# Alternating two attentions of one layer in one pipeline, stick-breaking by sigmoids and running products in the softmax pipeline, and head norm inside the output projection

## The chip, the cores and the metric

The kernel runs on one core of a Trainium2 chip. The time is the device time of one execution in microseconds (us). Before the change three executions gave 2448.42, 2451.39 and 2452.55, so the median is 2451.39. The core has five engines that run their own instruction lists in order and meet only at semaphores: TensorE (PE) for matmuls and transposes, VectorE (DVE), ScalarE (ACT), GpSimd (POOL), and SyncE (SP), which issues the transfers.

## The reference

A sequence of 512 tokens with 1024 features passes a first block (window attention with RWKV, then a gated feed-forward part) and two more layers. Each of these has a mixer, an output projection with a residual, and a feed-forward part. Layer 0 has the even mixer, layer 1 the odd mixer. Only the mixers and the projections behind them matter here.

```python
# even mixer: 8 forgetting heads (64 wide), 4 differential heads (values 128 wide)
s = q @ k.T * scale + (c[q] - c[k]);  p = softmax(causal(s));  o_a = p @ v
p = softmax(causal(q1 @ k1.T * scale)) - lam * softmax(causal(q2 @ k2.T * scale))
o_b = rms_norm_2(p @ v, subln) * (1.0 - lam_init)      # per head: x*rsqrt(mean(x*x)+EPS)*g
out = concatenate([o_a, o_b]) @ w_out

# odd mixer: 8 heads over keys picked by an indexer (softmax), 8 stick-breaking heads
z = q @ k.T * scale;  mask = key < query
log1m = where(mask, log_sigmoid(-z), 0)
after = reverse_cumsum(log1m) - log1m
a = where(mask, exp(log_sigmoid(z) + after), 0);  o_d = a @ v
out = concatenate([o_c, o_d]) @ w_out
```

## The kernel before

Everything lies in SBUF with features on the 128 partitions and tokens along the free axis (S = 512, P = 128, HD = 64). Weights stream in as fp32 tiles (`raw`), which ACT copies to a rounded part (`whi`, L309) and POOL subtracts to a rest (`wlo`, L313). Each product with weights is then three matmuls (L326 to L328). The program is a row of stages. In a stage each engine has a list written out by hand, and a stage ends with a handover by the engines' sequencers.

`attend` (L1020) runs attention over units. A unit is one pair of maps (two heads, or the two maps of one differential head) and one block of 128 queries; its keys are the blocks up to its own, so the width w goes 128, 256, 384, 512 and starts again. There are 16 units for 8 heads in pairs, or for 4 differential heads. In iteration i the engines do this, in this order:

- PE: scores of unit i (L1066), once the fused step of i-2 has left that pair of banks. Then it multiplies the weights of unit i-4 by the values (L1078), once ACT has copied them. Then it transposes the weights of unit i-3 (L1089), once they are normalised and the same copy is made.
- DVE: for forgetting units a masking add on the last block (L1102), then for each map a fused step that adds the bias, scales and takes the row maximum (L1106). Then the reciprocal of unit i-1's row sums (L1112), for differential units the merge of the two maps of i-2 (L1118), and the copy of a finished output (L1123).
- ACT: two exponentials of unit i (L1134), then the copy of unit i-3's transposed weights out of PSUM (L1143).
- POOL: normalises both maps of a unit (L1043), or, for a differential unit, scales the second map (L1048).

Even mixer (`even_mixer`, L2017): first 16 forgetting units, then as another stage 16 differential units, whose outputs go to `ob`. Then `norm` (L420) as a stage of its own: squares on ACT (L432), means by matmuls with a column of ones (L393), square root and reciprocal, spreading by matmuls (L402), and two DVE steps per head (L2054, L2055) into `oT`. Then `project_out` (L717), whose `Cut` (L546) splits the eight slices of `oT` (L554 on ACT, L559 on DVE) before eight output tiles follow, each of 24 matmuls and a residual add (L772). The feed-forward part follows.

Odd mixer (`odd_mixer`, L2196): PE makes keys and values from the latent (L2227, L2230), ACT and DVE copy them out (L2246). One `attend` of 16 units follows. `turn` (L1145) transposes the values of the stick-breaking heads. `stick_breaking` (L2257) then works head by head on blocks of keys by queries, 1280 columns in all: scores (L2282) copied out by ACT (L2319), softplus from three passes on ACT over 1280 columns (L2322 to L2324) and one on DVE (L2354), the running sum over keys by matmuls with a triangle and with ones (L2292, L2294), subtraction and clamp (L2347, L2349), exponential (L2328), masking (L2356, L2361), values (L2303) and copy (L2333). `project_out` then begins again with the split.

## Time and profile before

The profiled execution took 2450.87 us; its span in the profile is 2449.0 us. All times of the trace count from the start of that span. The mean granted clock of PE was 0.953.

| stretch | from | to | us |
|---|---|---|---|
| forgetting units | 1164.55 | 1222.56 | 58.0 |
| differential units | 1222.56 | 1270.06 | 47.5 |
| head norm, up to the first split of `project_out` | 1270.06 | 1287.40 | 17.3 |
| `project_out` of the even layer up to its last residual add's start | 1287.40 | 1335.52 | 48.1 |
| picked-key softmax units | 1871.1 | 1922.0 | 50.9 |
| transposes of the stick-breaking values | 1922.0 | 1927.0 | 5.0 |
| stick-breaking | 1927.0 | 2013.2 | 86.2 |

Over the whole span PE is busy 92% of the time, DVE 50%, POOL 40% and ACT 35%. The rows further down are of four kinds. A timeline row has a start, a duration (both us), the engine, the line, what is written and read, and a count; in brackets stands how long the engine was idle before and what released it. A row of the view by windows has a stretch, its length, busy time and count for PE, PEld (weight load), DVE, ACT and POOL, then the granted clock (1 is full), the share of the DMA engines and GB/s. A row of the groups by line has the count, busy time and mean duration, and the idle time before. A row of the view of one line has shortest, median and longest duration in ns, and first and last start.

### The profile page before, as it was taken

What the parts mean: (1) busy time and instruction counts of PE and PEld (TensorE: products, weight loads), DVE (VectorE), ACT (ScalarE), POOL (GpSimd) and SP (SyncE); (2) the same over time, 40 slices, a digit from 0 to 9 for tenths busy, and PEclk for the clock granted to TensorE, in tenths of its full rate; (3) what the DMA queues carried; (4) which work ended last, traced back from release to release, by engine and by line L of the source; (5) the groups of instructions that cost most, each with busy time, mean ns of one, the idle gap of its engine ahead of it and who ended that gap; (6) DMA issues with size and microseconds to landing.
All of it is one profiled execution on the core that took longest, in us unless ns stands there. A gap on an engine that the chain in (4) does not pass through costs nothing. (4 is left out here: it accounts for less than half of the span.)

```text
span 2449.0 us, 35685 instructions
## 1 busy us (share of the span) xinstructions
PE 2250.8 (92%) x13345; PEld 1805.7 (74%) x13345; DVE 1230.1 (50%) x2004; ACT 869.4 (35%) x1337; POOL 973.3 (40%) x507
## 2 busy tenths in 40 slices
PE   6995997799999999899778999999998799999998
PEld 4674986588788888777567888877786557888876
DVE  3337425777406761515453677711695362677601
ACT  3443223433213332432543333322324563333322
POOL 4322111344444444466523344444466204344442
PEclk8996998899999999999778999999999899999999
DMA  4220011233323333233002233233231003233332
GB/s 127 61 61 15 4 33 47 60 102 95 102 82 96 90 102 103 66 86 86 1 1 80 76 102 94 84 95 105 73 87 44 1 1 95 78 103 94 90 94 82
DMA packets 347229, 177.16 MB, mean 72 GB/s; under 512 B 20851, under 2 KB 344302, under 8 KB 347118
## 3 DMA queue, kind: packets, MB, share of 16 engines
q1 hardware_dynamic: 346620, 175.53, 25.1%
q8 instruction: 74, 1.21, 0.2%
q14 instruction: 37, 0.30, 0.0%
q10 hardware_dynamic: 210, 0.08, 0.0%
q0 software_dynamic: 288, 0.03, 0.0%
HBM read 173.51 MB, written 2.11 MB: 72 GB/s over the span
## 5 line engine op out<-in xcount | busy, mean ns | idle before, releaser
L313 POOL TENSOR_TENSOR wlo<-raw,whi 128x1024 fp32r<-128x1024 f32 (+3 forms) x347 | 793.9, 2292 | 1226.3 <-ACT whi L818 645.2
L326 PE MATMUL banks<-xhi,whi 128*128 128x512 f32 x1688 | 670.7, 397 | 5.9 <-DVE cb L977 3.9
L328 PE MATMUL banks<-xhi,wlo 128*128 128x512 f32 x1688 | 660.4, 391 | 0.0
L327 PE MATMUL banks<-xlo,whi 128*128 128x512 f32 x1688 | 660.3, 391 | 0.0
L326 PEld LDWEIGHTS banks<-xhi,whi 128*128 128x128 f32 x1688 | 319.2, 189 | 81.9 <-issue 12.7
L327 PEld LDWEIGHTS banks<-xlo,whi 128*128 128x128 f32 x1688 | 319.3, 189 | 69.0 <-issue 3.6
L328 PEld LDWEIGHTS banks<-xhi,wlo 128*128 128x128 f32 x1688 | 318.8, 189 | 67.1
L818 ACT ACTIVATE whi<-raw 128x1024 fp32r<-128x1024 f32 (+1 forms) x216 | 209.7, 981 | 191.6 <-DMA raw<-in_ffn_w_out_dram 84.5
L906 ACT ACTIVATE cb<-banks,conv 128x512 f32<-128x512 f32 x152 | 118.1, 779 | 446.0 <-DVE banks L966 446.0
L326 PE MATMUL banks<-ghi,whi 128*128 128x512 f32 x608 | 238.7, 393 | 19.7 <-DVE xT L1008 13.8
L327 PE MATMUL banks<-glo,whi 128*128 128x512 f32 x608 | 237.2, 390 | 0.0
L328 PE MATMUL banks<-ghi,wlo 128*128 128x512 f32 x608 | 237.1, 390 | 0.0
L966 DVE TENSOR_TENSOR banks<-banks,rs 128x512 f32<-128x512 f32 x152 | 106.3, 700 | 184.9 <-PE banks L328 168.5
L985 DVE CAST ghi<-gv 128x512 f32 (+1 forms) x76 | 168.4, 2216 | 9.0
L326 PEld LDWEIGHTS banks<-ghi,whi 128*128 128x128 f32 x608 | 114.5, 188 | 49.3 <-issue 17.9
L309 ACT ACTIVATE whi<-raw 128x1024 fp32r<-128x1024 f32 (+3 forms) x131 | 128.0, 981 | 34.1 <-PE banks L328 17.6
L328 PEld LDWEIGHTS banks<-ghi,wlo 128*128 128x128 f32 x608 | 114.5, 188 | 24.1
L327 PEld LDWEIGHTS banks<-glo,whi 128*128 128x128 f32 x608 | 114.6, 188 | 23.4
L977 DVE SCALAR_TENSOR_TENSOR cb<-banks,conv,cb 128x510 f32<-128x510 f32 x152 | 113.8, 749 | 18.3 <-DVE cb L975 0.3
L1008 DVE TENSOR_TENSOR xT<-banks,xT 128x512 f32 x16 | 11.1, 692 | 209.1 <-PE banks L328 209.1
L975 DVE SCALAR_TENSOR_TENSOR cb<-banks,conv,cb 128x511 f32<-128x511 f32 x152 | 112.7, 741 | 4.2 <-ACT cb L906 4.2
L1043 POOL TENSOR_SCALAR ex<-ex,mx 128x128 f32<-128x128 f32 (+3 forms) x64 | 68.3, 1085 | 37.6 <-DVE mx L1112 37.6
(446 smaller groups left out, 2730.5 us busy)
## 6 DMA issues: line engine op xcount, KB each, us to landing
raw<-in_ffn_w_in_dram SPq DMA_DIRECT2D x88, 512.0 KB, 3.9
raw<-in_w_ffn_up_dram SPq DMA_DIRECT2D x64, 512.0 KB, 4.1
raw<-in_w_ffn_down_dram SPq DMA_DIRECT2D x32, 512.0 KB, 4.2
raw<-in_ev_w_in_dram SPq DMA_DIRECT2D x25, 512.0 KB, 4.0
raw<-in_ffn_w_out_dram SPq DMA_DIRECT2D x32, 384.0 KB, 3.6
raw<-in_ffn_w_out_dram SPq DMA_DIRECT2D x32, 320.0 KB, 3.2
raw<-in_od_w_in_dram SPq DMA_DIRECT2D x20, 512.0 KB, 3.8
raw<-in_w_in_dram SPq DMA_DIRECT2D x16, 512.0 KB, 3.8
```

The costliest lines, as they stand in the source:

```text
L309: w_hi.by(act.activation(whi[s % CUT][:, 0:n, :], raw[s % RAW][:, 0:n, :], ACT.Copy))
L313: return pool.tensor_tensor(wlo[c][:, 0:n, :], raw[b][:, 0:n, :], whi[c][:, 0:n, :].bitcast(F32), ALU.subtract)
L326: pe.matmul(acc, whi[b][:, k, :], hi(k), start=first and k == 0, stop=False)
L327: pe.matmul(acc, whi[b][:, k, :], lo(k), start=False, stop=False)
L328: mm = pe.matmul(acc, wlo[b][:, k, :], hi(k), start=False, stop=last and k == n - 1)
L818: act.activation(whi[s % CUT][:, 0:n, :], raw[s % RAW][:, 0:n, :], ACT.Copy).then_inc(w_hi.h, 1)
L906: act.activation(cb[j][:, :], bank[j][:, :], ACT.Identity, scale=conv[:, 2, bass.ds(c, 1)], bias=conv[:, 3, bass.ds(c, 1)])\
L966: dve.tensor_tensor(bank[j % 4][:, :], bank[j % 4][:, :], rs, ALU.mult).then_inc(scaled.h, 1)
L975: chain(dve.scalar_tensor_tensor(cb[j][:, 1:S], bank[j][:, 0:S - 1], conv[:, 1, bass.ds(c, 1)], cb[j][:, 1:S], ALU.mult, ALU.add))
L977: dve.scalar_tensor_tensor(cb[j][:, 2:S], bank[j][:, 0:S - 2], conv[:, 0, bass.ds(c, 1)], cb[j][:, 2:S], ALU.mult, ALU.add).then_inc(conve ...
L985: dve.tensor_copy(ghi[:, i * 2 + q, :], gv[q][:, :]).then_inc(upper.h, 1)
L1043: ins = pool.tensor_scalar(e[:, g, 0:w], e[:, g, 0:w], mx[u % 4][:, 2, g:g + 1], None, ALU.mult)
```

## The change

1. Even mixer: one `attend` of 32 units, in which forgetting unit (j, n) and differential unit (j, n) alternate. Values are now multiplied five iterations behind the scores, not four (SUM). A unit's transposed weights always lie in banks 4 and 5. ACT's copy stands at the head of the next iteration (COPY = 4). Differential outputs go straight to `oT`.
2. Head norm: the stage is gone. Inside `project_out` the first two output tiles go slice by slice over `oT`, while the last four slices are squared (DVE), averaged over the partitions by a matmul with a square of ones, put through a logarithm and an exponential (ACT, this gives gain * rsqrt), multiplied (DVE) and split.
3. Odd mixer: the values of the stick-breaking heads are transposed in the stage that makes keys and values. Then one `attend` has the 16 softmax units and 16 stick-breaking units behind them. A stick-breaking unit has queries on the partitions, as the softmax ones do. DVE adds the mask in PSUM, ACT takes sigmoid(-z) and sigmoid(z) straight from PSUM, DVE makes the running product of sigmoid(-z) from the last key to the first (one scan for each head, reading and writing backwards), and POOL multiplies sigmoid(z) by the product of one key further. From there it is transposed, copied and multiplied by the values like the others.

```diff
+    class HeadNorm:
+        TILES = 2
...
+        def mean(self, pe, h):
+            pe.wait_ge(self.squared.h, h + 1)
+            pe.matmul(bank[4 + h][:, :], ones, self.sq[:, h, :], start=True, stop=True).then_inc(self.summed.h, 1)
...
+            for k in range(KD):
+                pe.wait_ge(self.ready.h, k + 1)
+                for m in range(self.TILES):
...
+                for h in {1: [0], 2: [1], 3: [2, 3]}.get(k, []):
+                    self.mean(pe, h)
...
+            for k in range(4):
+                self.upper(act, k)
+            split_hi(act, s0 + AHEAD)
+            act.wait_ge(self.set.h, 2)
+            for h in range(5):
+                if h < 4:
+                    x = self.sq[:, h, :]
+                    act.wait_ge(self.summed.h, h + 1)
+                    chain(act.activation(x, bank[4 + h][:, :], ACT.Ln, scale=1.0 / P, bias=self.const[:, 0:1]))
+                    act.activation(x, x, ACT.Exp, scale=-0.5, bias=self.const[:, 1:2]).then_inc(self.rooted.h, 1)
+                if h >= 1:
+                    act.wait_ge(self.normed.h, h)
+                    self.upper(act, 3 + h)
...
-        SETS, TURN, SUM = 2, 3, 4
+        SETS, TURN, COPY, SUM = 2, 3, 4, 5
...
+                    if x.sticking:
+                        pool.wait_ge(scanned.h, sticks.index(u) + 1)
+                        normed.by(pool.tensor_tensor(e[:, :, 0:w - 1], e[:, :, 0:w - 1], rest[u % 2][:, :, 1:w], ALU.mult))
...
-                        pe.wait_ge(normed.h, u + 1)
-                        free = u if heads == 2 else u - 1
-                        if free >= 1:
-                            pe.wait_ge(ptaken.h, free)
+                        wait_weights(pe, u)
+                        if u >= 1:
+                            pe.wait_ge(ptaken.h, u)
...
+                            for g in range(2):
+                                back = sm[u % 2][:, g, 0:w][:, ::-1]
+                                ins = dve.tensor_tensor_scan(rest[u % 2][:, g, 0:w][:, ::-1], back, back, 1.0, ALU.mult, ALU.min)
+                            scanned.by(ins)
...
+                            z = banks[:, b0:b0 + 2, 0:w]
+                            act.activation(sm[i % 2][:, :, 0:w], z, ACT.Sigmoid, scale=-HD ** -0.5)
+                            ins = act.activation(ex[i % 4][:, :, 0:w], z, ACT.Sigmoid, scale=HD ** -0.5)
...
-            norm(lambda k: ob[:, k, :], 4, 2 * HD, EPS, finish, groups=4)
...
-            stick_breaking(sq_, sk_, sv_, past, after, oT)
```

PE in the even attention. `ak`, `aq`, `vta` belong to forgetting units, `bk`, `bq`, `vtb` to differential ones; `ex` to transpose, `pt` to multiply by values. Before:

```order
L1089 MATMUL banks<-cst,ex_305 128x128 x6
L1066 MATMUL banks<-ak,aq 128x256 x2
L1066 MATMUL banks<-ak,aq 128x128 x2
L1078 MATMUL banks<-pt_307,vta 64x128 x6
L1089 MATMUL banks<-cst,ex_306 128x128 x8
L1066 MATMUL banks<-ak,aq 128x256 x4
L1078 MATMUL banks<-pt_308,vta 64x128 x8
```

and in the changed program:

```order
L1146 MATMUL banks<-cst,ex_307 128x128 x6
L1123 MATMUL banks<-ak,aq 128x128 x2
L1135 MATMUL banks<-pt_312,vtb 128x128 x2
L1146 MATMUL banks<-cst,ex_308 128x128 x3
L1123 MATMUL banks<-bk,bq 128x128 x2
L1135 MATMUL banks<-pt_311,vta 64x128 x6
```

The kinds alternate, and each product with values (now L1135) belongs to a unit that was copied one iteration earlier than before.

ACT from the end of the even attention on. `sq<-ob` are the squares of the norm stage, `hi<-oT` the split, `whi` a weight tile. Before:

```order
L432 ACTIVATE sq<-ob 128x512 x4
L408 ACT_TABLE_LOAD
L408 ACTIVATE st<-st 128x16
L151 UNCONDITIONAL_BRANCH
L751 UNCONDITIONAL_BRANCH
L554 ACTIVATE hi<-oT 128x512 x8
L309 ACTIVATE whi_14<-raw_10 128x1024
```

and in the changed program:

```order
L708 ACTIVATE hi<-oT 128x512 x4
L308 ACTIVATE whi_14<-raw_10 128x1024
L720 ACT_TABLE_LOAD
L720 ACTIVATE headsq<-banks,headconst 128x512
L721 ACT_TABLE_LOAD
L721 ACTIVATE headsq<-headsq,headconst 128x512
L720 ACT_TABLE_LOAD
L720 ACTIVATE headsq<-banks,headconst 128x512
L721 ACT_TABLE_LOAD
L721 ACTIVATE headsq<-headsq,headconst 128x512
L708 ACTIVATE hi<-oT 128x512
```

The logarithm (L720) and the exponential (L721) each have a table load in front, for each of the four heads, and the fifth split stands behind two heads' worth of them.

DVE in stick-breaking. Before, one head in its steady state:

```order
L2347 TENSOR_TENSOR aw_479<-zs_474,banks 128x512
L2349 TENSOR_SCALAR aw_479<-aw_479 128x512
L2347 TENSOR_TENSOR aw_479<-zs_474,banks 128x384
L2349 TENSOR_SCALAR aw_479<-aw_479 128x384
L2347 TENSOR_TENSOR aw_479<-zs_474,banks 128x256
L2349 TENSOR_SCALAR aw_479<-aw_479 128x256
L2347 TENSOR_TENSOR aw_479<-zs_474,banks 128x128
L2349 TENSOR_SCALAR aw_479<-aw_479 128x128
L2354 SCALAR_TENSOR_TENSOR sp_478<-zs_475,sp_478 128x1280
L2356 TENSOR_TENSOR sp_478<-sp_478,past 128x128 x4
```

and in the changed program two units:

```order
L1158 TENSOR_TENSOR banks<-banks,own 128x2x128
L1179 SCALAR_TENSOR_TENSOR rest_455<-sm_443 128x384 x2
L1194 COPY oT<-banks 128x128
L1158 TENSOR_TENSOR banks<-banks,own 128x2x128
L1179 SCALAR_TENSOR_TENSOR rest_456<-sm_444 128x512 x2
L1194 COPY oT<-banks 128x128
```

The listing names the scans of L1179 by their operand form. A unit's mask comes one iteration ahead of the scans of the unit before it.

## Rows read from the trace of the kernel before

**Rows 1.** View by windows: forgetting units, differential units, stick-breaking.

```profile
1161.90:1222.60 60.70, 44.85 (x337) 31.49 (x336) 28.94 (x116) 30.55 (x81) 34.19 (x32) 0.78 0.00 1
1222.60:1270.10 47.50, 36.85 (x216) 27.59 (x216) 27.20 (x112) 24.70 (x80) 13.04 (x16) 0.79 0.00 1
...
1926.90:2010.50 83.60, 74.80 (x281) 46.15 (x282) 49.67 (x136) 57.57 (x72) 0.00 (x0) 0.94 0.00 1
```

**Rows 2.** Timeline, forgetting units: two period marks, and one link of the chain.

```profile
1184.38 0.44 PE L1089 MATMUL banks<-cst,ex 128*128 128x128 f32 x2
...
1189.19 0.92 PE L1066 MATMUL banks<-ak,aq 64*128 64x256 f32 x8
...
1190.16 0.43 DVE L1102 TENSOR_TENSOR banks<-banks,mask 128x256 f32<-128x256 f32 x1 [0.86 <-PE banks L1066]
1190.63 0.56 DVE L1106 CUSTOM_DVE_ANT_0 sm<-banks,f 128x384 f32<-128x384 f32 x1
...
1191.71 0.61 ACT L1134 ACTIVATE ex<-sm,mx 128x384 f32<-128x384 f32 x1 [0.85 <-DVE mx L1106]
...
1192.92 1.00 ACT L1143 ACTIVATE pt<-banks 128x1024 f32<-128x1024 f32 x1
...
1193.97 1.09 PE L1078 MATMUL banks<-pt,vta 128*64 128x128 f32 x16
...
1195.00 0.44 PE L1089 MATMUL banks<-cst,ex 128*128 128x128 f32 x2
```

**Rows 3.** Timeline, transposes of differential units: two period marks.

```profile
1240.05 0.27 PE L1089 MATMUL banks<-cst,ex 128*128 128x128 f32 x1
...
1249.10 0.27 PE L1089 MATMUL banks<-cst,ex 128*128 128x128 f32 x1
```

**Rows 4.** Groups by line: the copies of the forgetting, then the differential stage.

```profile
L1143 ACT ACTIVATE pt<-banks 128x256 f32<-128x256 f32 (+3 forms) x16 | 11.1, 692 | 9.8 <-PE banks L1089 9.7
...
L1143 ACT ACTIVATE pt<-banks 128x128 f32<-128x128 f32 (+3 forms) x16 | 6.8, 423 | 6.2 <-PE banks L1089 6.2
```

**Rows 5.** Timeline: first and last period mark of the forgetting units, and last copy.

```profile
1169.06 0.33 PE L1089 MATMUL banks<-cst,ex 128*128 128x128 f32 x1
...
1208.06 0.44 PE L1089 MATMUL banks<-cst,ex 128*128 128x128 f32 x2
...
1269.77 0.29 DVE L1123 COPY ob<-banks 128x128 f32<-128x128 f32 x1 [3.32 <-PE banks L1078]
```

**Rows 6.** Timeline: head norm and the start of the even layer's output projection.

```profile
1272.57 1.28 ACT L408 ACT_TABLE_LOAD   x1
...
1287.40 3.23 ACT L554 ACTIVATE hi<-oT 128x512 fp32r<-128x512 f32 x6 [8.91 <-PEq L151]
...
1290.32 0.63 PE L326 MATMUL banks<-hi,whi 128*128 128x512 f32 x1
```

**Rows 7.** Timeline, odd layer: last period mark, value transposes, start of the output projection.

```profile
1908.32 0.44 PE L1089 MATMUL banks<-cst,ex 128*128 128x128 f32 x2
...
1922.37 3.65 PE L1157 MATMUL banks<-cst,sv 128*128 128x128 f32 x16 [0.66 <-PEq L151]
...
2013.51 3.23 ACT L554 ACTIVATE hi<-oT 128x512 fp32r<-128x512 f32 x6 [0.28 <-PEq L151]
```

**Rows 8.** View of one line each: scan, residual add, addition of two SBUF tiles, POOL product.

```profile
L1246 DVE TENSOR_TENSOR_SCAN tmp<-inside,cs x4: 1224/1224/1226, 192.1 to 197.0; 128x512 f32<-128x512 f32 x4
...
L772 DVE TENSOR_TENSOR xT<-banks,xT x8: 691/692/692, 1297.4 to 1335.5; 128x512 f32<-128x512 f32 x8
...
L614 DVE TENSOR_TENSOR bk<-bk,rotated x3: 692/2696/2698, 1149.0 to 1161.6; 128x512 f32<-128x512 f32 x3
...
L650 POOL TENSOR_TENSOR bk<-bk,rs x4: 1265/1298/1307, 1140.2 to 1159.7; 128x512 f32<-128x512 f32 x4
```

**Rows 9.** Timeline of POOL and DVE at the same moment, two inputs in SBUF each.

```profile
1148.27 2.85 POOL L313 TENSOR_TENSOR wlo<-raw,whi 128x1024 fp32r<-128x1024 f32 x1
...
1148.97 2.70 DVE L614 TENSOR_TENSOR bk<-bk,rotated 128x512 f32<-128x512 f32 x1
```

More of the change, by code:

```diff
@@ L719, in project_out @@
+    def project_out(oT, scale, mixed=None, make_side=None, gain=None):
         s0, n = state["s"], KD
@@ L741, in _ @@
             def _(pe):
-                for m in range(n):
+                if gain:
+                    lead.pe(pe, s0)
+                for m in range(lead.TILES if gain else 0, n):
                     s = s0 + m
@@ L752, in _ @@
             def _(act):
-                lead.act(act)
+                if gain:
+                    lead.act(act, s0)
+                else:
+                    lead.act(act)
                 for m in range(n):
-                    split_hi(act, s0 + m + AHEAD)
+                    if not gain or m >= AHEAD:
+                        split_hi(act, s0 + m + AHEAD)
                     if m >= 3:
@@ L766, in _ @@
                 chain = Chain(dve, dve_chain)
-                lead.dve(dve, None)
+                if gain:
+                    lead.dve(dve)
+                else:
+                    lead.dve(dve, None)
                 for m in range(n + 1):
@@ L1069, in _ @@
                     if 0 <= u < U:
-                        values = units[u][3]
+                        x = units[u]
                         pe.wait_ge(ptaken.h, u + 1)
@@ L1073, in _ @@
                             pe.wait_ge(otaken.h, u - 1)
-                        last = len(values) - 1
-                        for b, v in enumerate(values):
-                            for g in range(heads):
-                                r0, r1 = (g * HD, (g + 1) * HD) if heads == 2 else (0, P)
+                        last = len(x.values) - 1
+                        for b, v in enumerate(x.values):
+                            for g in range(x.heads):
+                                r0, r1 = (0, P) if x.paired else (g * HD, (g + 1) * HD)
                                 mm = pe.matmul(bank[6 + u % 2][r0:r1, 0:P], v[:, r0:r1], pt[u % 2][:, g, b * P:(b + 1) * P],
@@ L1103, in _ @@
-                        if i >= 2:
-                            dve.wait_ge(exped.h, i - 1)
-                        for g in range(2):
-                            ins = dve.tensor_tensor_reduce(sm[i % 2][:, g, 0:w], bank[b0 + g][:, 0:w], bias[g], -HD ** -0.5,
-                                                           3e38, ALU.add, ALU.min, mx[i % 4][:, 0, g:g + 1])
-                        ready.by(ins)
+                        if x.bar is not None:
+                            z = banks[:, b0:b0 + 2, w - P:w]
+                            ins = dve.tensor_tensor(z, z, x.bar.rearrange("p (o n) -> p o n", o=1).broadcast_to([P, 2, P]), ALU.add)
+                            if x.sticking:
+                                barred.by(ins)
+                            else:
+                                chain(ins)
@@ L1110, in _ @@
                     if 0 <= u < U:
[L1111 to L1118 removed]
+                        x, w = units[u], units[u].w
@@ L2246, in _ @@
                             act.activation(dv[:, t, :, :].rearrange("p m n -> p (m n)"), bank[4 + t][:, :], ACT.Copy)
+                        for t in range(NT):
+                            act.wait_ge(flipped.h, t + 1)
+                            act.activation(vt[:, t, :, :].rearrange("p m n -> p (m n)"), bank[t][:, :], ACT.Copy)
                 units = []
@@ new lines, in odd_mixer @@
+                        units.append(Unit([(cq[p0:p0 + HD, j, n * P:w], dk[p0:p0 + HD, j, 0:w]) for p0 in (0, HD)], w,
+                                          [dv[:, b, j, :] for b in range(n + 1)], oT[:, j, n * P:w],
+                                          bias=[future[:, :] if n == 0 else keep[:, n - 1, 0:w]] * 2))
+                for j in range(4):
+                    for n in range(NT):
+                        w = (n + 1) * P
+                        units.append(Unit([(sq_[p0:p0 + HD, j, n * P:w], sk_[p0:p0 + HD, j, 0:w]) for p0 in (0, HD)], w,
+                                          [vt[:, b, j, :] for b in range(n + 1)], oT[:, 4 + j, n * P:w],
+                                          bar=own[:, :], sticking=True))
```

371 lines of the change are left out of this document (136 added, 235 removed).

## The prediction

> **What bounds the kernel now.** I looked first at the busy shares: PE works 92% of the span, so whatever does not touch the stages where PE waits can be worth little. The view by windows then shows where it waits: PE is busy for 44.85 of 60.7 us in the forgetting units, at a mean clock of 0.78, and for 36.85 of 47.5 us in the differential ones. In stick-breaking it is busy for 74.80 of 83.6 us at 0.94 [rows 1]; there PE's own work is the bound, and only taking work away helps. The weights cost nothing here: the DMA share is 0.00 in all three [rows 1], their buffers being full. The change touches these stages, the head norm and the seams, nothing else.
>
> In the attention no engine is full, so I read the timeline for a chain. The reader should follow one link [rows 2]: scores at 1189.19, masking add 0.97 later, fused steps 0.47 on, exponentials 1.08 on, copy 1.21 on, product with values 1.05 on, transposes 1.03 on, and then the next scores but one. Two such links, of 128 and 384 columns, make the period of four units, 1184.38 to 1195.00, 10.62 us [rows 2]. Differential units need 9.05 [rows 3].
>
> **Even attention.** Before, it takes 1164.55 to 1270.06, 105.5 us (table above, and [rows 5]). After, the chain through a forgetting unit no longer holds the product with values (its weights were copied an iteration earlier), and its copy is that of a differential unit. Per eight units, four of each kind, this chain is 2 x 10.62, less 2.7 for products (1.03 for 16 matmuls [rows 2], 40 in four widths, about 2.6), less 1.1 for copies (11.1/4 against 6.8/4 [rows 4]): 17.4 us. The chain through the differential units is 2 x 9.05 - 2.7 + 1.1 = 16.5. Both run beside each other, where before 10.62 + 9.05 = 19.7 were needed. PE's work is (44.85 + 36.85)/4 = 20.4 us per eight units at a mean clock of 0.78 [rows 1], some 16 at full clock. So PE is nearly as long as the chain, and the two chains must collide on it. I take 19.0, between 17.4 and 20.5. The steady gain is small; what is saved above all is a ramp, a drain and their low clock.
>
> The sum: ramp 4.5 as before (1164.55 to 1169.06 [rows 5]); three periods, 57.0; low clock at the start and one dip, 6.7 (the three forgetting periods took 1169.06 to 1208.06, 39.0 instead of 31.9 [rows 2, 5]); a tail of 17. The old forgetting tail was 14.5 for four units (1208.06 [rows 5] to 1222.56), the new one has eight, half of them at the steady pace. Together 85.2, so **-20.3**; with a tail of 15 to 20 and the two bounds on the period -27 to -10. That ACT copies at the head of an iteration instead of at the end of the one before changes nothing by itself: its list reads copy, exponentials, copy in both programs. Cost nothing.
>
> **Head norm.** Before, the end of attention to the last residual add of `project_out` takes 1270.06 to 1335.5, 65.5 us [rows 5, 8]. After, the first splits start 0.6 into the stage and four last 2.2 (3.23 for six [rows 6]). PE works on slices 0 and 1 at once, at low clock, where a matmul is 0.63 long [rows 6] instead of about 0.39: 12 matmuls and the first mean, done at about 8 us. Now ACT is the chain. The order shows a table load before each logarithm and each exponential. The trace has a load at 1.28 [rows 6], and an exponential of 512 columns is about 0.75 (0.61 for 384 [rows 2]): 4.1 us for a head. Two heads stand before the fifth split, so slice 4 is ready at about 18.4, slice 5 at 24, slice 7 at 29.5. PE waits meanwhile and falls to low clock. With slice 7 of both tiles at 32 and six tiles of 5.44 each (seven intervals between the adds, 1297.4 to 1335.5 [rows 8]), plus the add, the end is at 67.0: **+1.6**. The removed stage of 17.3 us is thus paid back by the waits inside the projection. Bounds: -2 if the first table load runs while ACT would wait, +4 if PE stays slow for two tiles. One more table load stands in the next feed-forward part; I cost it at nothing, since ACT waits there, 1.28 if not.
>
> The trace has the load right behind the squares and the next thing 1.28 later [rows 6], with no pause around it. The Trainium skill ("ScalarE: Activation LUTs", What ACT_TABLE_LOAD costs) gives a drain of about 1380 ns on top for each switch; by it eight loads would cost 21 us instead of 10, and the head norm would come to about +12. The same page (Table sets: the hidden batching unit) names a set with both functions, by which one load would do; the order shows eight, so this stays a remedy and not a forecast.
>
> **Odd mixer.** Before, 1871.1 to 2013.2, 142.1 us (table above). After:
> The value transposes move ahead, 3.65 at low clock [rows 7], and with their copies on ACT add 3.4.
> The softmax units reach the last period mark 37.2 us in (1908.32 [rows 7]). The product with values leaves this chain too, 2.7/2 per four units, three times: 33.4. From there the first stick-breaking scores, table load, sigmoids and the first scan take 5.6 more: 39.0.
> Then the pace of stick-breaking units. Scans: 1224 ns for 512 columns [rows 8], 2560 columns in four units, about 6.5 us. POOL's product: 1.27 to 1.30 for 512 columns [rows 8], 2552 columns, 6.3. Masks and output copies of DVE 2.9. PE about 8, ACT 8.3 (three passes over two heads' columns at 11.1/4 [rows 4]). What decides is whether DVE and POOL can run together: where both had two inputs in SBUF, the DVE addition took 2.70 beside a POOL subtraction of 2.85 and ended 0.55 after it; alone it takes 0.69 [rows 8, 9]. It waited. So scans and products take turns, 12.8 + gaps: **14 us for four units**, 56 in all.
> An end of 4.4. The sum is 102.8: **-39.3**.
> The bounds of the pace are 10 (no exclusion) and 17 (the masks and copies take turns as well, 14 + 2.9). No row shows a scan that reads backwards; I take the forward price, since the number of columns is the same.
>
> The Trainium skill ("SBUF — State Buffer", Who interferes with whom) has it that DVE with two SBUF inputs contends with a GpSimd operation that reads SBUF, by a lock held for a whole instruction. By that rule a mask or a copy from PSUM stays free and the pace is the 14 above.
>
> **Sum.** -20.3 + 1.6 - 39.3 = -58.0. Against 2450.87 of the profiled execution this gives 2392.9; the median of 2451.39 is 0.5 away and changes nothing.
>
> **The rivals.**
> 1. *Scans and products overlap.* Then DVE (9.4) or ACT sets the pace, 10 us for four units: 16 less, **2377**. For: the scan is given the same tile twice, not two. Against: rows 9.
> 2. *PE bounds the alternating units.* If the clock stays at 0.78, PE needs 20.4 per eight units and meets the chains on top, about 22: +10, **2403**. For: collisions and rows 1. Against: at 90% busy the clock was 0.94 in stick-breaking [rows 1].
> 3. *The table loads weigh otherwise.* One load instead of eight would save 9 (**2384**). A pause of the size of the load around each would cost 10 (**2403**).
> 4. *Slower than before.* The backward scans run at a fraction of the forward pace. They cost 6.5 of the 14; each extra microsecond counts four times. The gain is gone when the pace is 28.5, which is when the scans take 21, over three times the forward price. At four times, pace 33.5, it ends at **2471**. Against: nothing in the trace speaks for a direction; the nearest stretching, the addition beside POOL, is waiting and already counted.
> 5. *It does not do what it says:* the units alternate but each kind still waits for the other's copy. Then only ramp and drain are saved: **2400**; the order shows the freed product, so this lies in the range.
>
> **How the numbers follow.** Forecast 0.50, rival 1 0.18, rival 2 and 5 0.19, rival 3 0.09, rival 4 0.03, something else near no change 0.01. The forecast is that of the likeliest, 2393. Its own terms span 2380 to 2410; rival 1 and a good even attention reach to 2368, rival 2 with the skewed norm to 2415. What a measurement can tell from no change is about 0.2%, 5 us. All but rival 4 and one in a hundred are faster than that: faster 0.96, same 0.01, slower 0.03.
>
> **What will show it.** In the profile after: the period of eight alternating units (19), the end of this stage about 85 us after its start; eight table loads near the logarithms and a gap of PE before slices 4 to 7; the period of four stick-breaking units (14), with no POOL product running beside a scan at its price of alone; 3.4 more before the odd attention. If the pace of stick-breaking is 10 or 20, or the alternating period over 21, the step that failed is that one.

## The result, and the profile after

The changed kernel takes 2372.45 us (median of four executions, 2370.76 to 2378.02), the kernel before 2451.57 beside it. The ratio is 0.9683, with a 95% interval from 0.9665 to 0.9702: 79 us less, where 58 were forecast. 2372 lies in the stated range, 20 us below the forecast of 2393.

The profiled execution, with 2378.02, is the slowest of the four. Up to the even attention, where the two programs do nearly the same, it is already 3.7 us later than the profile of before (first scores at 1168.28, not 1164.55). So stages are compared here from their own starts, and a second profile of the same kernel (`again`, below) stands beside it.

The page of the changed kernel begins:

```profile
span 2376.2 us, 35610 instructions
## 1 busy us (share of the span) xinstructions
PE 2192.9 (92%) x13337; PEld 1767.4 (74%) x13337; DVE 1219.5 (51%) x1928; ACT 856.7 (36%) x1328; POOL 993.1 (42%) x523
```

PE has lost 58 us of busy time (2250.8 before), its share stays 92%.

Windows of the changed kernel: even attention, then the stick-breaking units with the last softmax units. The columns are those of [rows 1].

```profile
1168.30:1249.50 81.20, 69.31 (x524) 50.02 (x524) 52.05 (x222) 53.02 (x160) 46.56 (x48) 0.87 0.00 1
...
1886.00:1941.00 55.00, 41.13 (x410) 29.50 (x408) 45.15 (x74) 36.32 (x59) 26.51 (x20) 1.00 0.00 1
```

In [rows 1] PE was busy for 74% and 78% of the even attention's two stages at a clock of 0.78 and 0.79; now it is 85% at 0.87. In stick-breaking PE was the bound (74.80 of 83.6); now it is busy for 75%, and DVE, with 45.15 of 55.0, is the fullest engine. Part of DVE's busy time turns out to be waiting (below).

| stretch | before | forecast | after | `again` |
|---|---|---|---|---|
| even attention, first scores to last copy | 105.5 | 85.2 | 84.7 | 81.6 |
| end of it to the last residual add of the projection | 65.5 | 67.1 | 62.5 | 62.4 |
| value transposes, moved ahead (what the stage of keys and values grew by) | | +3.4 | +2.0 | +2.0 |
| odd attention, start to first stick-breaking scan | | 39.0 | 39.6 | 39.6 |
| from there to the last output copy | | 60.4 | 50.2 | 50.2 |
| odd attention in all, with the transposes | 142.1 | 102.8 | 91.8 | 91.8 |

So the even attention came out as forecast (and 3.1 us better in the second profile), the head norm 4.6 us better, the odd layer 11 us better. One term, the pace of the stick-breaking units, has all of that last difference; the other terms of the odd layer cancel. The three stretches are 77.3 us shorter in `again`, and its whole profiled execution (2374.10) is 76.8 shorter than that of before.

### The profile page after: what moved, and what is told of

Its sections match the earlier page's. It is cut to its first block and busy times, and to the rows that moved or that the text cites. A ratio compares the mean times of both kernels' runs of the same rounds, so it can differ in the third digit from the quotient of the medians.

```text
span 2376.2 us, 35610 instructions
## 1 busy us (share of the span) xinstructions
PE 2192.9 (92%) x13337; PEld 1767.4 (74%) x13337; DVE 1219.5 (51%) x1928; ACT 856.7 (36%) x1328; POOL 993.1 (42%) x523
## 5 line engine op out<-in xcount | busy, mean ns | idle before, releaser
L325 PE MATMUL banks<-ghi,whi 128*128 128x512 f32 x608 | 239.3, 394 | 19.7 <-DVE xT L1046 13.8
L1015 DVE SCALAR_TENSOR_TENSOR cb<-banks,conv,cb 128x510 f32<-128x510 f32 x152 | 113.8, 749 | 18.3 <-DVE cb L1013 0.3
L1046 DVE TENSOR_TENSOR xT<-banks,xT 128x512 f32 x16 | 11.1, 692 | 209.1 <-PE banks L327 209.1
```

Of the source, the lines that this page charges most:

```text
L325: pe.matmul(acc, whi[b][:, k, :], hi(k), start=first and k == 0, stop=False)
L1015: dve.scalar_tensor_tensor(cb[j][:, 2:S], bank[j][:, 0:S - 2], conv[:, 0, bass.ds(c, 1)], cb[j][:, 2:S], ALU.mult, ALU.add).then_inc(conve ...
```

## The experiments

All times are medians of four executions, beside runs of the kernel before on the same chip. Four such sets of the kernel before gave 2448.74, 2448.80, 2449.99 and 2451.53 us, the first and the last of them on one chip. So differences under 3 us between two kernels are read from stages, not from medians. The granted clock of one stretch also changes from run to run: the odd layer's softmax units take 35.5 us up to the first stick-breaking scores in some profiles with five iterations (clock 0.90) and 33.5 in others (clock 1.00), though nothing was edited there.

### The changed kernel again

> The changed kernel once more, unchanged, so that the other runs have a neighbour on the same chip. Expected: 2372 us, between 2369 and 2378, ratio to the kernel before 0.968. In the profile: even attention 84.7 us, period of four stick-breaking units 11.15 us, last residual add of the even output projection 62.5 us after the end of attention.

Measured: 2373.38 us, ratio 0.9689 (0.9673 to 0.9705). From first scores to first split of the even layer it takes 81.9 us, and the period of eight alternating units is read from the transposes of the first differential unit of each head:

```profile
1192.70 0.27 PE L1146 MATMUL banks<-cst,ex 128*128 128x128 f32 x1
...
1211.38 0.27 PE L1146 MATMUL banks<-cst,ex 128*128 128x128 f32 x1
```

18.7 us, where 19.0 was taken. The other profile had one such period and one of 19.9.

### One table load in the head norm

```diff
             act.wait_ge(self.set.h, 2)
+            act.preload_act_table_set("natural_log_exp_and_others")
             for h in range(5):
```

> The changed kernel with one explicit load of the table set that holds logarithm and exponential before the first logarithm of the head norm, in place of eight loads. Theory (ACT's loads are the chain between the first four slices and the last four): each head costs 1.4 us on ACT instead of 4.0, the last slice comes about 9 us earlier, and PE, which waits for it, ends 9 us earlier: 2363 us. Rival (PE or the squares are the bound there, the loads being hidden): under 2 us, 2371. If every load brought a pause of about its own length, the gain would be nearer 18, 2354.

Measured: 2360.81 us, ratio 0.9650 (0.9630 to 0.9670), 12.6 less than `again`. From the first split to the first residual add it takes 19.5 us (1244.9 to 1264.4) where `again` takes 28.7 (1247.0 to 1275.7): 9.2 less, the theory's 9. The other 3 us lie outside this stage; in the profiles 2.1 of them have come before the even attention. This is how ACT looked in the changed kernel; start, duration, engine, line:

```profile
1260.27 1.28 ACT L720 ACT_TABLE_LOAD   x1 [3.84 <-PE banks L690]
...
1261.56 0.69 ACT L720 ACTIVATE headsq<-banks,headconst 128x512 f32<-128x512 f32 x1
...
1262.27 1.28 ACT L721 ACT_TABLE_LOAD   x1
...
1263.56 0.72 ACT L721 ACTIVATE headsq<-headsq,headconst 128x512 f32<-128x512 f32 x1
...
1264.30 1.28 ACT L720 ACT_TABLE_LOAD   x1
...
1269.75 0.79 PE L699 MATMUL banks<-hi,whi 128*128 128x512 f32 x1 [4.22 <-DVE lo L730]
...
1277.64 0.72 ACT L721 ACTIVATE headsq<-headsq,headconst 128x512 f32<-128x512 f32 x1
```

A head costs 4.03 (1260.27 to 1264.30), PE waits 4.22 for the fifth slice, and each load of 1.28 is followed by its activation 1.29 after its start. There is no pause. From the first load to the end of the last exponential ACT needs 18.1 (1260.27 to 1278.36). With the single load, that load runs where ACT would wait, and the two activations of a head stand back to back:

```profile
1248.06 1.28 ACT L716 ACT_TABLE_LOAD   x1
...
1250.25 0.69 ACT L721 ACTIVATE headsq<-banks,headconst 128x512 f32<-128x512 f32 x1 [0.90 <-PE banks L690]
...
1252.49 0.69 ACT L721 ACTIVATE headsq<-banks,headconst 128x512 f32<-128x512 f32 x1 [0.80 <-PE banks L690]
...
1255.31 0.67 ACT L721 ACTIVATE headsq<-banks,headconst 128x512 f32<-128x512 f32 x1
1256.01 0.73 ACT L722 ACTIVATE headsq<-headsq,headconst 128x512 f32<-128x512 f32 x1
1256.64 0.61 ACT L708 ACTIVATE hi<-oT 128x512 fp32r<-128x512 f32 x1
```

The one load that is left ends before ACT's wait for the first mean, so all eight are off the chain, which is 10.2. Of these 0.80 goes into a new wait for PE's mean of the second head, and 0.6 into PE (from the end of the last exponential to the first add 5.8 us, 5.2 in `again`); 8.8 are left by this count, 9.2 measured. So the theory's 9 is right in size, not as a count of loads. The Trainium skill ("ScalarE: Activation LUTs", What ACT_TABLE_LOAD costs) puts about 1380 ns of drain on top of each load; an estimate by that is 21 us for the eight loads alone, more than the whole 18.1. The measurement decides: here a load costs 1.28 and nothing more.

### Stick-breaking without POOL's product

The weight of key k is R(k+1) - R(k), with R the running product. So the sum over values is the last value plus the sum of R(k) (v(k-1) - v(k)).

```diff
-                            act.activation(sm[i % 2][:, :, 0:w], z, ACT.Sigmoid, scale=-HD ** -0.5)
-                            ins = act.activation(ex[i % 4][:, :, 0:w], z, ACT.Sigmoid, scale=HD ** -0.5)
+                            ins = act.activation(sm[i % 2][:, :, 0:w], z, ACT.Sigmoid, scale=-HD ** -0.5)
...
-                                ins = dve.tensor_tensor_scan(rest[u % 2][:, g, 0:w][:, ::-1], back, back, 1.0, ALU.mult, ALU.min)
+                                ins = dve.tensor_tensor_scan(ex[u % 4][:, g, 0:w][:, ::-1], back, back, 1.0, ALU.mult, ALU.min)
...
+                            otaken.by(dve.tensor_scalar(units[u].out, bank[6 + u % 2][:, 0:P], units[u].lastv, None, ALU.add))
...
+                        dve.tensor_tensor(sd[:, :, 1:S], sv_[:, :, 0:S - 1], sv_[:, :, 1:S], ALU.subtract).then_inc(keyed.h, 1)
```

> The changed kernel without POOL's product in stick-breaking. Weight k is the running product from k+1 minus that from k, so the sum over values is taken as the running products times differences of neighbouring values, plus the last value: ACT takes one sigmoid, DVE's scan writes what is transposed, two DVE operations make the differences ahead (about 3 us, in the stage of keys and values), and the output copy adds the last value. Theory (a scan with two inputs in SBUF and POOL's product take turns, so that their times add: 6.0 + 5.25 = 11.2 us for four units): without the product DVE alone sets the pace, scans 6.0, masks 1.8, copies 1.2, about 9.2 us, four times 2 us less and 2 to 3 more for the shorter tail, less about 2 for the differences: 2364 us. Rival (the pace of 11.15 is the chain of scores, mask, sigmoids and scan, POOL overlapping): pace stays above 10.5, 2371 to 2375 us.

Measured: 2366.29 us, ratio 0.9660 (0.9644 to 0.9676), 7.1 less than `again`, where the theory had 9. The period is 9.24, as it said (9.2). From the first stick-breaking scores to the split it takes 46.1 us, 54.7 in `again`: 8.6 less. The projection behind takes 48.2 to its last add at a clock of 0.93, 45.3 at 1.00 in `again`. This is DVE (and POOL) in the changed kernel, around a unit of 512 columns and the next of 128:

```profile
1910.85 1.19 DVE L1179 TENSOR_TENSOR_SCAN rest<-sm 128x512 f32<-128x512 f32 x1
1911.96 0.26 DVE L1194 COPY oT<-banks 128x128 f32<-128x128 f32 x1
1912.12 1.99 POOL L1099 TENSOR_TENSOR ex<-ex,rest 128x1022 f32<-128x1022 f32 x1 [2.28 <-DVE rest L1179]
1912.14 0.42 DVE L1158 TENSOR_TENSOR banks<-banks,own 128x256 f32<-128x256 f32 x1
1912.47 2.23 DVE L1179 TENSOR_TENSOR_SCAN rest<-sm 128x128 f32<-128x128 f32 x2
```

and this is DVE without the product:

```profile
1902.71 0.42 DVE L1159 TENSOR_TENSOR banks<-banks,own 128x256 f32<-128x256 f32 x1
1903.04 0.73 DVE L1180 TENSOR_TENSOR_SCAN ex<-sm 128x128 f32<-128x128 f32 x2
...
1906.83 0.43 DVE L1159 TENSOR_TENSOR banks<-banks,own 128x256 f32<-128x256 f32 x1 [1.07 <-PE banks L1124]
...
1911.94 0.42 DVE L1159 TENSOR_TENSOR banks<-banks,own 128x256 f32<-128x256 f32 x1
```

The same two scans of 128 columns take 2.23 with a product running beside them and 0.73 without. The product runs from 1912.12 to 1914.11; the scans end at 1914.70, 0.59 behind it. The profile has the first scan as begun at 1912.47, with no wait for a semaphore before it; it ends only behind the product. The mask (1912.14, one input in SBUF, the other in PSUM) runs in its usual 0.42 at the same time. That is what the Trainium skill has ("SBUF — State Buffer", Who interferes with whom): two inputs in SBUF against a POOL operation that reads SBUF, for whole instructions; and the trace agrees with it on the mask, too.

One half of the theory does not hold: DVE does not set the new pace alone. It is idle for 1.07 of the period, until the scores of the 512-column unit are there. PE, at full clock, is the fuller engine (the columns are those of [rows 1]):

```profile
1902.50:1911.70 9.20, 8.55 (x85) 6.18 (x84) 8.13 (x17) 5.33 (x8) 0.00 (x0) 1.00 0.01 3
```

### The product twice

```diff
+                        junked.by(pool.tensor_tensor(junk[:, :, 0:w - 1], e[:, :, 0:w - 1], rest[u % 2][:, :, 1:w], ALU.mult))
                         normed.by(pool.tensor_tensor(e[:, :, 0:w - 1], e[:, :, 0:w - 1], rest[u % 2][:, :, 1:w], ALU.mult))
```

> The changed kernel with POOL's product of each stick-breaking unit done twice, the first time into a tile that nobody reads. Theory (scans and products take turns, their times add): period of four stick-breaking units 11.15 + 5.25 = 16.4 us, 21 us more in all, 2394 us. Rival (they overlap and POOL has slack, 5.25 of 11.15 busy): doubled it is busy for 10.5 of 11.15, period up to 12, under 4 us more, 2377 us.

Measured: 2396.07 us, ratio 0.9783 (0.9767 to 0.9800), 22.7 more than `again`. Period marks of the changed kernel, then of the doubled one:

```profile
1906.74 0.41 PE L1146 MATMUL banks<-cst,ex 128*128 128x128 f32 x2 [0.38 <-ACT pt L1205]
...
1917.89 0.41 PE L1146 MATMUL banks<-cst,ex 128*128 128x128 f32 x2 [0.38 <-ACT pt L1205]
```

```profile
1902.86 0.41 PE L1149 MATMUL banks<-cst,ex 128*128 128x128 f32 x2 [0.44 <-ACT pt L1208]
...
1919.27 0.33 PE L1149 MATMUL banks<-cst,ex 128*128 128x128 f32 x1
```

11.15 against 16.41: the 5.25 of added POOL work is on the path as a whole, although POOL was busy for less than half of the time before. Together with the run before, this settles that scans and products take turns. It goes both ways. The first product of a unit (L1101) starts when DVE has just finished a scan; the second (L1102) finds the next scan begun. These are the groups of the two lines for 766 columns; the count, busy time and mean duration in ns stand in the middle:

```profile
L1102 POOL TENSOR_TENSOR ex<-ex,rest 128x766 f32<-128x766 f32 x4 | 9.8, 2456 | 0.0
...
L1101 POOL TENSOR_TENSOR junk<-ex,rest 128x766 f32<-128x766 f32 x4 | 6.2, 1545 | 6.1 <-DVE rest L1182 6.1
```

The same product takes 1.54 alone and 2.46 beside a scan.

### The forgetting units first

```diff
+                units = units[0::2] + units[1::2]
                 attend(units, lam=lam[:, 0:1])
```

> The changed kernel with the 32 units of the even attention in another order: the 16 forgetting units first, then the 16 differential ones, still in one pipeline with values five iterations behind. Theory (the gain of the even attention is the freed product with values and one ramp and drain less, and alternation adds nothing; two chains collide on PE): periods of 9.3 and 7.7 us for four units, 17 for eight, against 18.7 to 19.9 when alternating: 4 to 8 us less, 2366 us. Rival (alternation itself lets the short copies and transposes of one kind hide behind the long ones of the other, and POOL, 8.7 us for four forgetting units, is the bound when they stand together): 3 to 8 us more, 2378 us.

Measured: 2374.83 us, ratio 0.9697 (0.9681 to 0.9713), not to be told from `again` in time. Its stage is 1.9 longer (1157.24 to 1241.06, 83.8 us), and the projection behind it 1.6 longer from the first split to the first add (30.3 and 28.7). Both theories missed. Forgetting units, then differential units:

```profile
1185.78 0.44 PE L1146 MATMUL banks<-cst,ex 128*128 128x128 f32 x2
...
1196.34 0.44 PE L1146 MATMUL banks<-cst,ex 128*128 128x128 f32 x2
```

```profile
1214.94 0.27 PE L1146 MATMUL banks<-cst,ex 128*128 128x128 f32 x1
...
1223.48 0.27 PE L1146 MATMUL banks<-cst,ex 128*128 128x128 f32 x1
```

10.56 and 8.54, 19.1 for eight. The forgetting period was expected at 9.3. What follows is read from the order of the lists and not tried by itself. A link goes from a unit to the unit after the next. With four widths in a row one chain has the links of 128 and 384 columns, the other those of 256 and 512. The second is longer, and since the units alternate, the period is that of the slower. Alternating the kinds puts all four widths of a kind in one chain. So its 18.7 would be the chain through the forgetting units. Alternation is worth 0.4 us per eight units, by this reading because it balances the links.

### Four iterations instead of five

```diff
-        SETS, TURN, COPY, SUM = 2, 3, 4, 5
+        SETS, TURN, COPY, SUM = 2, 3, 4, 4
```

> The changed kernel with the product with values four iterations behind the scores again, as before the change; alternation, the single pipeline and everything else stay. Theory A (the prediction's: the fifth iteration takes the product with values off the chain, 2.7 us for eight units): 11 us more in the even attention (81.9 to 93), 4 more in the softmax units of the odd layer, in all 2388 us. Theory B (PE must run a product between one unit's scores and the next transposes in either case, so that only its wait moves; the even attention's gain is the one ramp and drain less, with their low clock): 2 us more in the even attention, 1 to 2 in the odd one, 2375 to 2378 us.

Measured: 2395.06 us, ratio 0.9774 (0.9753 to 0.9795), 21.7 more than `again`. Theory B falls; theory A has the stages, and a total 7 us too low.

```profile
1194.23 0.38 PE L1146 MATMUL banks<-cst,ex 128*128 128x128 f32 x2
...
1216.33 0.38 PE L1146 MATMUL banks<-cst,ex 128*128 128x128 f32 x2
```

The period of eight is 22.1 instead of 18.7, and the stage 93.6 us instead of 81.9 (theory A: 93). The odd softmax units take 38.7 instead of 35.5 up to the first stick-breaking scores, the units behind them 57.0 instead of 54.4. The last 4 us are not in these stages: 2.6 have come before the even attention, and 1.8 lie in its projection (30.5 instead of 28.7 to the first add).

Two things could have made the period longer: the chain of waits, and the lower clock that comes with them. The windows of one period, here and in `again`:

```profile
1194.23:1216.33 22.10, 17.62 (x140) 12.57 (x139) 13.47 (x56) 13.41 (x41) 11.86 (x13) 0.92 0.00 1
```

```profile
1192.70:1211.38 18.68, 15.94 (x140) 11.63 (x139) 13.13 (x57) 13.13 (x40) 11.65 (x12) 1.00 0.00 1
```

PE does the same work in 17.62 instead of 15.94, so the clock can account for at most 1.7 of the 3.4. The rest, at least half, is the chain.

### Two stages again, with five and with four iterations

```diff
-                attend(units, lam=lam[:, 0:1])
+                attend(units[0::2])
+                attend(units[1::2], lam=lam[:, 0:1])
```

> The changed kernel with the even attention in two stages again, forgetting units, then differential ones, each with values five iterations behind; everything else as in the changed kernel. It has the seam back, and no alternation. By the chain of the links the steady periods are those of the grouped order, 10.5 and 8.5 us for four units, so it differs from that order (83.9 us from first scores to first split) by the seam alone. Theory (the seam is most of what the even attention saved: one ramp of 4.5, one drain, and the low clock of PE after it): 12 to 16 us more, the stage pair takes 96 to 100 us and the kernel 2386 to 2390 us. Rival (the fifth iteration is what saved most, as its undoing cost 12 us when the kinds alternate): 4 to 7 us more than grouped, 2379 us.

Measured: 2383.06 us, ratio 0.9723 (0.9707 to 0.9739), 9.7 more than `again`, between the two theories. The stages take 90.7 us (1164.5 to 1255.2). That is 6.9 above the grouped order, so by the stages the rival is right: the seam is worth 7, not 12 to 16.

```profile
1164.30:1214.00 49.70, 39.13 (x336) 27.52 (x336) 26.13 (x112) 30.23 (x81) 34.12 (x32) 0.86 0.00 1
1214.00:1255.20 41.20, 32.95 (x216) 24.91 (x216) 26.41 (x113) 24.38 (x81) 12.98 (x16) 0.88 0.01 1
```

The same two stages took 58.0 and 47.5 us before, at clocks of 0.78 and 0.79 [rows 1]. So PE's clock rises already without the merging.

The same kernel with SUM back at 4:

> The changed kernel with the even attention in two stages and values four iterations behind the scores, as before the change in both; head norm in the projection and the odd layer's single pipeline stay, the latter with four iterations too. It separates the fifth iteration from the seam: two stages took 105.8 us before and 90.7 with five iterations. Theory (the fifth iteration alone is worth these 15): the two stages take 104 to 107 us from first scores to first split, and with the 6 us that four iterations cost in the odd layer the kernel takes 2403 to 2407 us. Rival (something else in the rewritten pipeline gave the 15, such as the place of ACT's copy or the banks): under 98 us, 2390 to 2396 us.

Measured: 2404.48 us, ratio 0.9806 (0.9782 to 0.9829), inside the theory's range. The two stages take 101.8 us (1168.8 to 1270.6), a little under it. Windows of this kernel; the first begins 1.8 before the first scores, and the borders are not exactly those of the stages:

```profile
1167.00:1222.00 55.00, 41.66 (x314) 28.94 (x315) 27.74 (x114) 29.47 (x80) 34.13 (x32) 0.77 0.00 1
1222.00:1270.00 48.00, 35.28 (x240) 26.52 (x238) 27.27 (x114) 25.61 (x81) 12.99 (x16) 0.89 0.00 1
```

Without the fifth iteration PE is back at a clock of 0.77 in the forgetting units. This gives the account of the even attention, from first scores to first split (or to the norm's squares, before):

| kernel | us | step |
|---|---|---|
| before | 105.8 | |
| `twofour`: two stages, four iterations | 101.8 | -4.0, not explained |
| `twostages`: two stages, five iterations | 90.7 | -11.1, the fifth iteration |
| `grouped`: one stage, in two groups | 83.8 | -6.9, the seam |
| `again`: alternating | 81.9 | -1.9, the alternation |

The 4.0 are not in the steady state. The forgetting stage agrees to 0.5 us, and the last two full periods of the differential stage together take 18.3 before and 18.2 in `twofour`. The difference lies at the ends of the differential stage: its first scores to first transposes (4.5 and 3.5), its first period (12.65 and 11.56), and its tail behind the last period mark (12.0 and 10.7).

### The even layer alone

The changed kernel with the odd layer's own value transposes and old stick-breaking in their stages:

```diff
+            turn([(vt[:, t, :, :], [v[:, m, t * P:(t + 1) * P] for m in range(4)]) for t in range(NT)])
...
+            stick_breaking(sq_, sk_, sv_, past, after, oT)
```

> The change of the even layer alone: alternating units and head norm inside the projection as in the changed kernel, with the odd layer as before (its own stage of value transposes, stick-breaking by softplus and triangle matmuls), except that its softmax units have the product with values five iterations behind. By the stages of the two profiles the even attention is worth 21 to 24 us, the head norm 3, the odd layer 50: expected 2449 - 27 + at most 2 = 2421 to 2425 us. Rival (the even layer's gain is partly lost later, in weights that come late to the projection): over 2430.

Measured: 2416.34 us, ratio 0.9858 (0.9839 to 0.9877), 32.5 below the kernel before, where 24 to 28 were expected. The even attention has its 81.9 us, the split to the first add 28.7, both as in `again`. What was underrated is the new `attend` in the odd softmax units:

```profile
1845.90:1890.00 44.10, 36.00 (x336) 25.53 (x336) 19.49 (x96) 30.16 (x81) 34.01 (x32) 0.96 0.01 1
```

Their stage takes 44.1 us, 50.9 before. Of these 6.8 us the fifth iteration is shown to be worth about 3.2 (its undoing cost 38.7 - 35.5). More than half of the 6.8 lie behind the last period mark: 1908.32 is 37.2 after the start before [rows 7], and the same mark comes at 34.1 here, so the steady part gave 3.1 and the stage's end 3.7. Over the softmax matmuls the clock is 0.88 before and 0.96 here. With 23.9 of the even attention and 3.0 of the head norm that is 33.7, against 32.5 measured. The rest of the odd layer's change is worth 2416.3 - 2373.4 = 43, between two chips.

### Faster versions

Both improvements together:

> The changed kernel with the single table load and with stick-breaking without POOL's product together. The two lie in different layers, so their gains add if nothing else is the bound: 2373.4 - 12.6 - 7.1 = 2354 us, ratio to the kernel before 0.961. Rival (one gives back part of the other's through the clock or the weights): 2358 or more.

Measured: 2356.16 us, ratio 0.9613 (0.9597 to 0.9629). Of the expected 19.7 it has 17.2, so they add within what runs on two chips can tell.

On top of both, the output copies of the stick-breaking units on ACT:

```diff
+                    u = i - SUM
+                    if 0 <= u < U and units[u].sticking:
+                        act.wait_ge(weighed.h, u + 1)
+                        otaken2.by(act.activation(units[u].out, bank[6 + u % 2][:, 0:P], ACT.Identity, bias=units[u].lastv))
```

> The kernel with the single table load and without POOL's product, and on top the output copies of the stick-breaking units on ACT in place of DVE. Theory (DVE is the bound of these units, 9.24 us for four, of which the copies are 1.1): period 8.1 to 8.5 us, 3 to 4 us less, 2352 us. Rival (the chain of scores, mask, sigmoid and scan binds as soon as DVE is relieved, or ACT's copy delays its next sigmoid): period above 9.0, 2356 us or more.

Measured: 2349.71 us, ratio 0.9591 (0.9575 to 0.9607), the fastest kernel of the study, 102 us below the one before. The reason given does not hold. The period went from 9.24 to 8.98, not to 8.3:

```profile
1889.97 0.73 DVE L1184 TENSOR_TENSOR_SCAN ex<-sm 128x128 f32<-128x128 f32 x2
...
1894.02 0.43 DVE L1163 TENSOR_TENSOR banks<-banks,own 128x256 f32<-128x256 f32 x1 [1.51 <-PE banks L1126]
...
1898.95 0.73 DVE L1184 TENSOR_TENSOR_SCAN ex<-sm 128x128 f32<-128x128 f32 x2
```

DVE now sits idle for 1.51 until the scores of the 512-column unit are there, where it had been idle for 1.07 without this edit: it was not the only bound before it either. The window of this period shows PE at 8.58 of 8.98:

```profile
1889.97:1898.95 8.98, 8.58 (x87) 6.19 (x86) 7.26 (x13) 6.34 (x12) 0.00 (x0) 1.00 0.01 3
```

With 8.6 of work for PE, at full clock, a period of 8.3 was out of reach. The stretch from the first stick-breaking scores to the split is 45.7 us, 46.1 in `both`. The projection behind it is 1.6 shorter, but at a clock of 1.00 against 0.96, and `again` has the same 45.3 there. So of the 6.4 us between the two medians only 0.4 is shown to be the edit's.

## Why the prediction was right, and where it was not

**The whole.** 58 us were forecast and 79 measured. The measured time lies in the range, 20 us from the forecast; 11.4 of these 20 are one term, the pace of the stick-breaking units.

**What bounds.** Right: the time went out of the stages in which PE waited and out of the triangle matmuls (the stretches named give 77.3 us in `again`, whose whole execution is 76.8 shorter).

**Even attention, -20.3 forecast, -20.8 and -23.9 in two profiles.** The sum and the period (19.0 taken, 18.7 measured) were right, the reason for the sum was not. "The steady gain is small; what is saved above all is a ramp, a drain and their low clock": the seam is worth 6.9, the fifth iteration 11.1. Two things hid this. The full-speed period of 10.62 in [rows 2] was one of three; the others, 15.3 and 13.1, were booked as low clock, which was put down to the start and to one dip. The runs with four and five iterations show that low clock comes with the waiting itself (0.77 against 0.86 in the forgetting units), and the two alternating ones that at least half of the longer period is waiting at full clock. And the chain of 17.4 came from a single period of before, doubled; the alternating units keep 18.7. The two errors lay in opposite directions, and so did two more in the sum. Ramp, three periods with their low clock, and tail were forecast at 4.5, 63.7 and 17; the first profile has 4.0, 60.4 and 20.3. That they meet at 84.7 is luck. (39.0 less 31.9 is also 7.1, not 6.7, so the prediction's own sum is 85.6.) That ACT's copy at the head of an iteration costs nothing was argued from the order and not tried by itself.

**Head norm, +1.6 forecast, -3.0 measured.** The mechanism was right, as the run with one load shows: ACT's chain of two loads and two activations per head, 4.1 forecast and 4.03 measured, decides. Two things made it come out too long. The sum does not add up: 32 and six tiles of 5.44 are 64.6 to the last add, 65.3 with the add, and not 67.0. By its own terms the forecast was -0.9, so 2.4 of the missed 4.6 us are a slip. The other 2.2 are the last slice, whose matmuls were done at 29.8 (forecast 32): the first logarithm's load started at 7.3 us (about 8), and the fifth slice was there at 16.8 (18.4). That PE would fall to low clock in its waits was true, but not in the same places. In the first profile slices 4 and 5 ran with matmuls 0.63 long and the last two with 0.39, in `again` slice 4, half of slice 5 and most of the last two with 0.63, and both took the same 62.4 to 62.5 us.

**Odd mixer, -39.3 forecast, -50.3 measured.** The value transposes cost 2.0, not 3.4: PE did them in 1.9 us at full clock, where [rows 7] had 3.65. The 39.0 to the first scan was right (39.6), in part by luck: the last period mark of the softmax units came at 35.1, not 33.4, and from there to the scan it took 4.5, not 5.6. In the four profiles in which the clock stayed full (`telescope`, `doubled`, `grouped`, `twostages`) the mark came at 33.1, so there the 33.4 was right. The step that failed is the pace: 14 taken, 11.15 measured, four times 2.85 = 11.4, which is the whole difference. Its mechanism was right; two terms of it were not. The product was priced at 1.27 to 1.30 for 512 columns from another line [rows 8]; it takes 1.09 for 510 and 1.99 for 1022. The view of its line:

```profile
L1099 POOL TENSOR_TENSOR ex<-ex,rest x16: 631/1314/1992, 1891.7 to 1934.4; 128x254 f32<-128x254 f32 x4, 128x510 f32<-128x510 f32 x4, 128x766 f32<-128x766 f32 x4, 128x1022 f32<-128x1022 f32 x4
```

That is 0.63 + 1.09 + 1.54 + 1.99 = 5.25 for four units, not 6.3; scans are 6.1, not 6.5 (and 6.1 is what 2560 columns make at the 1224 ns of [rows 8], so the 6.5 had no row behind it). And the 1.2 of gaps do not exist: 6.1 + 5.25 = 11.3 is the period of 11.15 to within 0.2, because masks and output copies run while the product holds the scans up. The backward scan costs what a forward one does (1.19 for 512 columns, 1224 ns in [rows 8]), as was assumed.

**The rivals.** Rival 1 (2377, scans and products overlap) is nearest in time and wrong in cause: doubling the product added all of it. Rival 2 did not come, since the clock rose to 0.88 and 0.92. Of rival 3 the saving by one load was real (9 forecast, 9.2 measured), and the pause does not exist. Rivals 4 and 5 fell.

**Open.** The 4.0 us between the kernel before and `twofour` in the same two stages. The differential stage has a clock of 0.89 there and 0.79 before, at nearly the same work; the banks of its transposes and where its outputs go were not tried by themselves. Also open is why POOL's product is faster than that of L650; the first of those, at 1140.24, ran 1.30 and no instruction of DVE with two inputs in SBUF began before 1141.47, so it was not held up by one. And no kernel relieved PE in the stick-breaking units, where it is the fuller engine once the product is gone.

## What to carry to other kernels

When an instruction of one engine sits between two others of a chain only because its own input is late, giving it one iteration more can be worth more than merging stages; undo it alone to see which of the two it was. Where DVE and POOL both read two tiles from SBUF, add their times, whatever POOL's busy share says, and look first for algebra that spares one of the two. Before relieving the engine that looks fullest, look whether it waits anywhere in the period, and how much work the next one has. Look in the list of ACT for table loads between two functions that one set holds: each is 1.28 us on the chain.

## What the runs showed of the hardware that was not expected

- A clock below full came with waits inside a steady pipeline, not only with ramps and drains: 0.77 with four iterations and 0.86 with five, the same matmuls in the same stage.
- A POOL product of two SBUF tiles took 1.09 us for 510 columns here and 1.27 to 1.30 for 512 on another line.
- Scans and products hold each other up in both directions: two scans of 128 columns took 2.23 instead of 0.73 beside a product, and a product of 766 columns 2.46 instead of 1.54 beside a scan.
- A DVE scan that is held up by POOL shows as a long instruction (2.23 for 0.73), not as idle time, so the views of waits say nothing of it. DVE's busy time in the changed kernel has these waits in it.
